# Moving the low parts of the gate weights from the vector engine to GpSimd in a single-core streaming encoder layer

## What is computed

```
u = rms_norm(x, g_pre)
q, k, v, z_a, q_g, k_g, v_g, z_g, lr, gate_A, gate_B = split(u @ w_in)
o_A = banded_attention(q, k, v, sinks)          # window of 128 tokens, softmax per head
o_B = gated_linear_attention(q_g, k_g, v_g, log_sigmoid(lr @ w_up + b) / 16)
y_A = (o_A * silu(z_a)) @ w_branch_attn
y_B = (rms_norm(o_B) * silu(z_g)) @ w_branch_gla
m   = sigmoid(gate_A + b_A) * y_A + sigmoid(gate_B + b_B) * y_B
out = x + rms_norm(m @ w_out, g_post)
```

## Time and profile before

| what | value |
|---|---|
| median of 3 runs | 3015.74 us |
| the profiled execution | 3015.31 us |
| its span, first to last instruction | 3013.5 us |
| PE busy, share of the span | 2839.3 us, 94% |
| DVE busy | 2021.3 us, 67% |
| ACT busy | 1166.0 us, 39% |
| POOL busy | 80.8 us, 3% |
| mean granted TensorE clock | 0.980 |

### The profile page before, as it was taken

One profiled execution on the slowest core, in us unless ns is written; L12 is line 12 of the kernel. 1 busy time (PEld: TensorE's weight loads), 2 busy tenths in 40 slices (PEclk: granted clock), 3 DMA queues, 4 the chain that ended last, 5 costly groups with the idle time before them and its releaser, 6 DMA issues.

```text
span 3013.5 us, 52534 instructions
## 1 busy us (share of the span) xinstructions
PE 2839.3 (94%) x20490; PEld 2682.8 (89%) x20490; DVE 2021.3 (67%) x3387; ACT 1166.0 (39%) x1908; POOL 80.8 (3%) x55
## 2 busy tenths in 40 slices
PE   7999999998999999998989989888789999999996
PEld 6999999998999999998777777766589999999996
DVE  7799777777687777776677766666553322455555
ACT  5334333344353333344455564544440000343331
POOL 0122000000000000000000000000000000000001
PEclk9999999998999999999999999999899999999998
DMA  3455343435344343445555555634373333556654
GB/s 115 135 189 189 120 129 120 135 117 207 107 134 137 125 131 122 127 128 155 161 165 153 163 164 162 176 113 130 103 233 108 118 121 108 169 174 194 190 182 147
DMA packets 227197, 441.10 MB, mean 146 GB/s; under 512 B 23840, under 2 KB 134688, under 8 KB 226096
## 3 DMA queue, kind: packets, MB, share of 16 engines
q1 hardware_dynamic: 226992, 438.31, 46.5%
HBM read 358.10 MB, written 80.67 MB: 146 GB/s over the span
## 4 chain that ended last, share of the span: by engine, by line
PE 69%; issue 12%; DVE 10%; ACT 4%; DMA 3%; POOL 1%; SPq 0%; DVEq 0%; ACTq 0%; POOLq 0%
PE bank L1751 37%; PE bank L1729 25%; DVE w_lo L1186 1%; PE bank L1914 1%; DVE w_lo L1165 1%; DVE s L1437 1%; DMA xs<-in_xT 1%; DMA w_raw<-in_w_tiles 1%; PE bank L1875 1%; ACT pb L960 1%; ACT w_hi L827 1%; PE bank L1761 1%; DMA gate<-o_scratch 1%; PE bank L1939 0%; PE bank L1944 0%
## 5 line engine op out<-in xcount | busy, mean ns | idle before, releaser
L1751 PE MATMUL bank<-th,w_hi 128*128 128x272 f32 x2400 | 701.4, 292 | 14.4 <-DVE w_lo L1186 7.8
L1751 PE MATMUL bank<-tl,w_hi 128*128 128x272 f32 x2400 | 696.2, 290 | 0.0
L1751 PE MATMUL bank<-th,w_lo 128*128 128x272 f32 x2400 | 695.7, 290 | 0.0
L827 ACT ACTIVATE w_hi<-w_raw 128x1024 fp32r<-128x1024 f32 x256 | 270.6, 1057 | 733.9 <-PE bank L1729 697.1
L1751 PEld LDWEIGHTS bank<-th,w_hi 128*128 128x128 f32 x2400 | 454.8, 190 | 19.6 <-DVE w_lo L1186 9.6
L1165 DVE TENSOR_TENSOR w_lo<-w_raw,w_hi 128x1024 fp32r<-128x1024 f32 x256 | 313.2, 1224 | 226.8 <-ACT w_hi L827 226.2
L1751 PEld LDWEIGHTS bank<-tl,w_hi 128*128 128x128 f32 x2400 | 454.9, 190 | 1.0 <-issue 1.0
L1751 PEld LDWEIGHTS bank<-th,w_lo 128*128 128x128 f32 x2400 | 454.4, 189 | 0.0
L850 ACT ACTIVATE w_hi<-w_more 128x1024 fp32r<-128x1024 f32 x240 | 254.5, 1061 | 474.7 <-DVE w_more L1205 254.2
L1186 DVE TENSOR_TENSOR w_lo<-w_more,w_hi 128x1024 fp32r<-128x1024 f32 x240 | 300.2, 1251 | 125.1 <-ACT w_hi L850 122.8
L1729 PE MATMUL bank<-uh,w_hi 128*128 128x272 f32 x1024 | 321.3, 314 | 5.8 <-DVE w_lo L1165 5.3
(11 more groups left out here) (208 smaller groups left out, 5058.8 us busy)
## 6 DMA issues: line engine op xcount, KB each, us to landing
w_raw<-in_w_tiles SPq DMA_DIRECT2D x376, 512.0 KB, 4.0
w_more<-in_w_tiles SPq DMA_DIRECT2D x120, 512.0 KB, 3.7
p_scratch<-stage SPq DMA_DIRECT2D x44, 544.0 KB, 3.0
gate<-gate_scratch SPq DMA_DIRECT2D x32, 544.0 KB, 3.9
gl<-p_scratch SPq DMA_DIRECT2D x8, 1536.0 KB, 10.4
qa<-p_scratch SPq DMA_DIRECT2D x8, 1152.0 KB, 8.1
gate_scratch<-stage SPq DMA_DIRECT2D x16, 544.0 KB, 3.1
gate_scratch<-stage SPq DMA_DIRECT2D x64, 136.0 KB, 3.9
```

The source lines that it names most:

```text
L827: act.activation(w_hi[:, h], w_raw[:, h], ACT.Copy).then_inc(s_whi, 1)
L1751: ins = pe.matmul(out[:, 0:GAW], wt[:, k], ut[:, k], start=start and k == 0 and i == 0, stop=stop and k == HK - 1 and i == 2, skip_group_c ...
```

## The change

GpSimd gets its own `lo_w`, with the same waits and the same instruction, and runs all 129 of them that lie in the attention stage; the vector engine's are taken out. To place them, GpSimd now walks through the same parts j as the other engines do, and `gla_roots` moves into that walk at step 22. Within a part the `lo_w` stands ahead of `gla_roots`. The first two, and with them the clears, stand ahead of the walk. The vector engine waits once for GpSimd's last one before it goes on with its own in the branch stage.

```diff
@@ gpsimd @@
+            def lo_w(p, h):
+                pool.wait_ge(s_whi, 2 * p + h + 1)
+                pool.tensor_tensor(w_lo[:, h], w_raw[:, h], w_hi[:, h].bitcast(f32), ALU.subtract).then_inc(s_wlo, 1)
+
+            lo_w(PASS_GATE, 0)
+            lo_w(PASS_GATE, 1)
             pool.wait_ge(s_mp, MIX_Q)
             pool.memset(st[:, 0], 0.0).then_inc(s_clr, 1)
             pool.memset(gsc[:], 0.0).then_inc(s_clr, 1)
-            gla_roots(0)
-            with pool.Fori(1, N_IT - 1) as it:
-                gla_roots(it)
-            gla_roots(N_IT - 1, DEC)
+
+            def attend(it, p, m0, count, nxt=True, again=None, fresh=False):
+                kts, nch, nq = shape_of(it)
+                for steps, j in weave(SUBS * count, it):
+                    m, h, sub = m0 + j // SUBS, j // 2 % 2, j % 2
+                    unit = N_LATE * p + m
+                    if sub == 0 and h == 1:
+                        lo_w(PASS_GATE + unit + 1, 0)
+                    elif sub == 0 and not (isinstance(unit, int) and unit == 0):
+                        lo_w(PASS_GATE + unit, 1)
+                    if 22 in steps:
+                        gla_roots(it, nq)
+
+            sequence(pool, attend)
@@ vector @@
-            lo_w(PASS_GATE, 0)
             dve.wait_ge(s_post, taken(MIX - 1, 6))
...
-            lo_w(PASS_GATE, 1)
             dve.wait_ge(s_bias, HEADS)
...
-                    if sub == 0 and h == 0:
-                        if not (isinstance(unit, int) and unit == 0):
-                            lo_w(PASS_GATE + unit, 1)
-                            if m > 0:
-                                scale_gate(unit - 1, p, m - 1)
-                            else:
-                                scale_gate(unit - 1, p - 1, N_LATE - 1)
-                    elif sub == 0:
-                        lo_w(PASS_GATE + unit + 1, 0)
+                    if sub == 0 and h == 0 and not (isinstance(unit, int) and unit == 0):
+                        if m > 0:
+                            scale_gate(unit - 1, p, m - 1)
+                        else:
+                            scale_gate(unit - 1, p - 1, N_LATE - 1)
...
+            dve.wait_ge(s_wlo, 2 * PASS_BRANCH + 1)
             lo_w(PASS_BRANCH, 1)
```

## The result

**Slower by 2.1%.** The changed kernel takes 3078.89 us (median of 4 runs, 3075.32 to 3079.61), the kernel before, run on the same chip, 3015.64 (4 runs, 3012.87 to 3017.17): ratio 1.0208, interval 1.0191 to 1.0226. The forecast was 3049, with a range up to 3074: the sign is right, the size is a little over half of what came, and the result lies outside the range. The profiled execution took 3079.15 us; its span is 3077.3 us.

The account below looks back on a forecast made before the run. PE was taken to bound the attention stage, hanging directly on DVE at the end of the softmax steps; 31 - 3 - 1 + 4 + 3 = +34 on 3015.31 us gave 3049 us, range 3018 to 3074.

Parts of the forecast that it names:

- 3 of slack: Softmax, two of nine blocks where PE does not wait for lac_lo: one hit of 1.5 us each absorbed, -3 us.
- the softmax term: Softmax steps: 42.0 us of nm waits plus 8.9 of snm waits less 20.0 of freed DVE time, +31 us.
- 28 hits of nm: Softmax: in 28 steps nm falls within POOL's 2.25 us and waits, 42.0 us together.
- 8.9 for snm on ties: Softmax: in 8 steps w_hi ends within 0.1 us of snm; half of 17.7 us waiting taken, 8.9 us.
- the 20 saved: Softmax, 72 steps: delay of den behind esink filled by DVE's w_lo, removed by the change, 20 us.
- Rival A: Softmax: short nm and snm are not held up, so the kernel gets faster, 2999 us; chance 0.10.
- B: Softmax: hits are partly absorbed, half of them (25 us) remaining, 3023 us; chance 0.13.
- C: Attention stage: POOL needs 2.69 us or more and cannot deliver in time, 3086 us and more; chance 0.10.
- the late hand-over, +7: Halves without steps (+4) and the twelve last parts (+3): POOL's longer w_lo delays what follows.
- my two upper bounds (8 and 6): Upper ends for halves without steps (0 to 8 us) and the twelve last parts (0 to 6 us).
- my +4: Step 22, six long blocks: roots queue behind POOL's w_lo, some 0.6 us later each, +4 us.
- the linear steps, -1: Linear attention: earlier ke gains 1.15 us, L1487 held up loses 1.09, nine times: -1 us, between -12 and +8.

Follow-up runs that it names:

- experiment 7: Changed kernel with POOL making only the low parts of the softmax steps (0 to 8), DVE the others: 3057.04 us.
- experiment 6: Changed kernel with POOL making only low parts from step 18 on and the last stretch: 3027.81 us; only those of steps 0 to 17: 3061.86 us.
- experiment 1: Changed kernel with POOL's low part covering only 8 of the 1024 columns, the tiny operation: 2984.08 us.
- Experiment 9: Kernel before, all low parts on DVE, zs moved from step 5 to 6: 3015.81 us; gate scaling and tanh also one part later: 2997.51 us.
- less writing: Changed kernel with POOL's low part reading 8 columns and writing 896 columns once, about 1.1 us: 2997.54 us.
- writes only: Changed kernel with POOL's low part cut to 8 columns, then two clears filling its old length: 3011.52 us.
- four pieces: Changed kernel with each low part on POOL as four instructions of 256 columns: 3068.04 us.
- placed, one piece: Changed kernel, POOL making only low parts of steps 0 to 17, each in one piece after waiting for a DVE result of that part: 3053.92 us.
- placed, two pieces: Changed kernel, POOL making only low parts of steps 0 to 17, in two 512-column pieces, each waiting for a DVE result of its part: 3080.02 us.
- before, with extra reader: Kernel before, low parts on DVE, plus 121 POOL subtractions of 1024 columns that nobody needs: 3168.69 us.

## Why the prediction was half right

**The parts add up.** Softmax parts +42.5 (experiment 7), linear attention parts +4.8 (6 less 7: 3061.86 - 3057.04, within the noise of the two), late parts +13 (6), later start of the stage +3.7: 64.0 us, measured 63.3. Forecast were +28 (31 less 3 of slack), -1, +7 and 0, together 34.

**Right in sum, with luck: the softmax term, as idle time of PE.** In the changed kernel: I had 28 hits of nm by 1.50 us, 42.0 us; there are 26, together 37.4. I had 8.9 for snm on ties; it is 2.1, one hit: in five steps snm and POOL's w_lo start within 0.02 us of one another, and DVE goes first in all five. Then come 4.8 us for den, 5.6 for pb and 1.4 for lac_lo, which I had not listed. 51.3 against 50.9, as waiting of DVE. Less the 20 saved and 3 of slack that makes 28; PE's idle time grew by 28.5 in experiment 7. But PE's waits say that this is two errors that cancel. In experiment 7 the waits of the softmax (pb, pT, lac_lo) grew by 22 us in all, and the rest is mostly w_lo coming late, 10.9 us for 5.3, which the term left out. In experiment 1, where nothing is added, the same three waits fell by 10 us, not 20. So of the 51 us of DVE's waiting some 32 reached PE (22 and 10, an estimate from two kernels), and of the 20 removed some 10: my reading that a longer softmax chain "arrives on PE nearly in full" was too strong both ways. Experiment 9 agrees: the 0.99 us of the step that I took as the model of the 20 lay in PE's slack. Rival A (short instructions are spared) is out: 1.66 us for one of 0.16. B, half the hits, is out as well (26 came where I had 28), though a part of each was absorbed; and so is C's premise (POOL at 2.69 us): it takes 2.38.

**Wrong: what a microsecond of idling costs.** The step that failed is the sum itself: "31 - 3 - 1 + 4 + 3 = +34 on the profiled 3015.31 us". It adds PE's new idle time to an execution whose busy time it takes as fixed. The idle time did grow by 38.2 us, near the 34. But PE's matmuls took 21.9 us more. The earlier trace rows gave the clock, 0.96, and I read it as a constant. How it acts is seen right behind the 7.3 us wait at the start of the stage, in windows and in PE's timeline:

```profile
1394.50:1396.50 2.00, 1.99 (x9) 2.00 (x10) 0.38 (x1) 1.39 (x2) 0.00 (x0) 0.50 0.00 0
1396.50:1398.50 2.00, 2.00 (x11) 1.67 (x12) 0.00 (x0) 0.38 (x1) 0.00 (x0) 0.50 0.63 236
1398.50:1400.50 2.00, 2.00 (x14) 1.78 (x11) 0.83 (x6) 0.23 (x1) 0.00 (x0) 0.52 0.91 253
1400.50:1402.50 2.00, 1.23 (x10) 0.93 (x8) 1.15 (x8) 0.75 (x5) 0.00 (x0) 1.00 0.66 190
```

```profile
1394.51 0.57 PE L1740 MATMUL bank<-uh,w_hi 128*128 128x272 f32 x1 [7.29 <-DVE stage L1414]
1394.87 0.43 PE L1740 MATMUL bank<-ul,w_hi 128*128 128x272 f32 x1
1395.10 0.43 PE L1740 MATMUL bank<-uh,w_lo 128*128 128x272 f32 x1
```

After the wait the clock is 0.50, 1.2 GHz, and matmuls of 272 columns start 0.23 us apart; from about 1400.4 on it is 1.00, 2.4 GHz, and they start 0.13 us apart in the same timeline. The kernel before is slow at its start too, behind its wait of 2.8 us: 0.50 from 1390.8 to 1392.8, 0.67 in the next 2 us, then 1.00. The Trainium skill, TensorE: Matmul & The Clock Gate, Part 1: The HAM clock gate, says that the slow rate is the resting state and that activity lifts it; the windows agree (0.50 behind 7.3 us of waiting, 1.00 at 1400.50). In the kernel before 9 waits of PE, those at both ends of the stage included, were over 2.5 us and 254 of its 3071 gate matmuls slow (over 0.38 us); now 13 and 350. Over the profiled executions the busy time goes with the idle time in both directions, with contention or without:

```
kernel                      length    busy    idle   (stage, us)
tiny operation               784.4   705.8    78.6
less writing                 792.9   709.8    83.1
zs and scaling moved         799.5   709.6    89.9
writes only                  810.3   715.7    94.6
zs moved                     815.5   716.7    98.8
before                       812.8   713.2    99.6
late parts only              829.0   719.0   110.0
softmax parts only           857.3   729.2   128.1
four pieces                  860.6   729.8   130.8
placed, one piece            853.1   721.6   131.5
early parts only             857.3   723.1   134.2
changed kernel               872.9   735.1   137.8
placed, two pieces           877.9   737.1   140.8
before, with extra reader    967.5   764.2   203.3
```

From the first row to the last it is 58.4 us of busy time for 124.7 of idle time, 0.47 for one. It isn't a fixed price: against the kernel before, 1 us more of idling comes with 0.26 (one piece) to 0.58 us (two pieces), and 1 us less gives back 0.2 to 0.4, but nothing in the kernel that only writes. Two kernels with the same idle time can differ by 3.5 us in busy time (zs moved, before). Which waits cost the clock and which don't, these runs leave open. At 0.5 for one, my 34 would have been 51, and 3066 us, within my range; with the late start, 3070. The whole sum is then 34 forecast, 4.2 of idle time more, 21.9 of slower matmuls and 3.7 of late start, 63.8 us.

**Mis-sized: the late hand-over, +7.** The late parts cost 13 us, near the sum of my two upper bounds (8 and 6). In the profiled execution of experiment 6 PE idles 10.4 us more in the stage and is busy 5.8 us longer (16 us together; what lies ahead of the stage and behind it came out 4 us shorter there), so a good part of the surplus is the clock again. Of the idle time, PE's wait for the scaled output grew by 4.1 us, my +4, though gmean (1112 ns on average in the changed kernel for 164), on the way to the roots, is held up too, which I had not thought of. In the twelve last parts it is not only the hand-over: bl, which splits the inputs of the branch products and has two inputs in SBUF, is held up three times in the changed kernel, and the last gate result waits behind it. No run separates the two.

```profile
2260.66 2.48 DVE L1566 TENSOR_TENSOR bl<-ya,bh 128x364 fp32r<-128x364 f32 x2 [1.36 <-ACT bh L1033]
```

Without POOL beside it such a pair takes 0.98 us.

**Missed: one-input instructions.** I wrote that "two instructions that both read two SBUF inputs exclude one another", and searched for nm, snm and the sums alone. The earlier trace rows had shown one DVE instruction beside POOL that was spared, and that one read PSUM. The TENSOR_SCALAR ones, bias, pb and gmean, with one tile to read and the output in SBUF, are held up too, and so is a COPY (ebend, 244 ns on average for 163). The late start comes from this; its 3.7 us are good to a microsecond or two, since the stage starts between 1388.7 and 1391.4 us in kernels that leave its start as it was.

**Inside its bounds, though by another way: the linear steps, -1.** Measured +5 by the medians and 0 by the stage's length, inside -12 to +8. I had expected L1501 to be hit (22 us of waiting, and it is) and wrote off qe and ke, which "no PE wait now shows"; ke waits 28.4 us in 13 hits. PE's wait for ke grew by only 6 us all the same. That w_lo no longer stands ahead of qe is a likely reason: without any contention, in experiment 1, the wait falls from 18.3 to 11.0 us.

## What to carry to other kernels

When work moves to GpSimd, list every DVE instruction with its operands in SBUF, one-input TENSOR_SCALAR ones too, and look at when the moved operation will start, not only at how long it takes: here 2.4 us of it beside a chain of 0.16 us instructions cost more than the 1.2 us that it freed. Add a term for TensorE's clock to a sum that is made of idle times: in this kernel each microsecond of idling brought a quarter to six tenths of a microsecond of slower matmuls, and each one saved gave at most 0.4 back. A hold-up of one engine is not yet idle time of the engine that bounds the kernel: look at the waits of that one. And before moving work to another engine, try another order on its own: zs and the gate's scaling at other places won 17 us, though zs alone won nothing.

## What the runs showed of the hardware that I had not expected

- **TENSOR_SCALAR is held up by a POOL that only writes.** With memsets on POOL gmean (128x4) takes 959 ns for 164 and pb 391 for 339, while nm and ke stay at 160 and 908. The Trainium skill, SBUF — State Buffer, Who interferes with whom, says both: that tensor_scalar can, on conditions, take the pair of ports that is shared, and that instructions with two inputs meet only POOL's reads. The runs agree on both.
- **A waiting POOL goes ahead of the next DVE instruction.** ke stands ready behind qe and still comes after POOL's w_lo, which asked during qe: 3.13 us for 0.95, thirteen times. The one hit of snm is of the same kind: POOL's w_lo asked while nm ran.
- **A hit costs the whole rest of the other's instruction**, whatever the length of one's own: nm, 0.16 us long, waits up to 1.9 us.
- **Four pieces of 256 columns take 802 ns each on average**, together 3.2 us beside DVE, for 2.42 us on average in one; two of 512 take 1.33 us each.
